# Twelve head pairs on one core: the copies of transposed keys move from SyncE's queue to GpSimd's

## The reference

```
h = rmsnorm(x, norm_g);  proj = h @ w_in          # q, k, v, gate of each group, forget logits
o_sb = stick_breaking_attention(q_sb, k_sb, v_sb)                       # causal
o_ch = chunked_relpos_attention(rmsnorm(q_ch), rmsnorm(k_ch), v_ch, rel_bias)   # own + 8 chunks of 64
o_fx = forgetting_attention(rmsnorm(q_fx), rmsnorm(k_fx), v_fx, log_sigmoid(f)) # causal
mixed = concat(o_sb * silu(g_sb), o_ch * silu(g_ch), o_fx * silu(g_fx))
out = x + mixed @ w_out
```

## Time and profile before

| | |
|---|---|
| device time, median of 3 runs | 1045.06 us |
| device time of the profiled execution | 1045.31 us |
| its span | 1043.5 us |
| PE busy | 1015.7 us, 97% |
| DVE, ACT busy | 682.6 us (65%), 632.2 us (61%) |
| POOL busy | 102.1 us, 10% |
| PE's share of the chain that ended last | 82% |
| copies stack<-stack, from issue to landing | 192 of 128 KB, median 2.3 us |

### The profile page before, as it was taken

One profiled execution on the slowest core, in us unless ns is written; L12 is line 12 of the kernel. 1 busy time (PEld: TensorE's weight loads), 2 busy tenths in 40 slices (PEclk: granted clock), 3 DMA queues, 4 the chain that ended last, 5 costly groups with the idle time before them and its releaser, 6 DMA issues.

```text
span 1043.5 us, 16263 instructions
## 1 busy us (share of the span) xinstructions
PE 1015.7 (97%) x5816; PEld 911.2 (87%) x5816; DVE 682.6 (65%) x1304; ACT 632.2 (61%) x1232; POOL 102.1 (10%) x90
## 2 busy tenths in 40 slices
PE   6999999999999999999999999999999998999998
PEld 6988989899899998998998998998998986787787
DVE  5656675765866667667557548879789787877100
ACT  6658775776767767758667667556567555553000
POOL 1210201101211011011012001011010010000000
PEclk9999999999999999999999999999999999999999
DMA  8254151431522513314314204204214228732941
GB/s 251 83 139 117 36 152 42 113 104 33 136 80 66 137 42 107 96 52 130 84 40 127 77 21 115 68 22 127 56 30 121 61 64 253 207 102 83 302 131 38
DMA packets 112944, 105.50 MB, mean 101 GB/s; under 512 B 10048, under 2 KB 83784, under 8 KB 112864
## 3 DMA queue, kind: packets, MB, share of 16 engines
q1 hardware_dynamic: 110784, 104.43, 36.3%
q10 hardware_dynamic: 2080, 0.04, 0.1%
HBM read 62.44 MB, written 19.98 MB: 79 GB/s over the span
## 4 chain that ended last, share of the span: by engine, by line
PE 82%; DVE 8%; DMA 4%; ACT 3%; issue 2%; SPq 0%; POOL 0%; ACTq 0%; DVEq 0%; POOLq 0%
PE psP L1216 37%; PE psO L1308 9%; PE psP L1220 8%; PE psT L1290 8%; PE psS L1268 4%; PE psS L1269 4%; PE psP L1356 2%; PE psS L1356 2%; PE psP L1326 2%; PE psT L1238 2%; PE psO L1356 2%; DVE big L1001 1%; DVE rb L1120 1%; PE psS L1273 1%; DMA stack<-mixed_scratch 1%
## 5 line engine op out<-in xcount | busy, mean ns | idle before, releaser
L1216 PE MATMUL psP<-big 128*128 128x384 f32 (+1 forms) x2304 | 478.5, 345 | 1.8 <-DVE big L1001 1.4
L1216 PEld LDWEIGHTS psP<-big 128*128 128x128 f32 x2304 | 394.9, 189 | 8.5 <-DVE big L1001 1.7
L1131 DVE TENSOR_TENSOR pt<-psT,pt 128x512 fp32r<-128x512 f32 (+1 forms) x224 | 143.4, 642 | 140.5 <-ACT pt L943 139.5
L943 ACT ACTIVATE pt<-psT 128x512 fp32r<-128x512 f32 (+1 forms) x224 | 125.1, 559 | 117.2 <-PE psT L1290 116.9
L1220 PE MATMUL psP<-big 128*128 128x512 f32 x576 | 157.1, 405 | 0.0
L1308 PE MATMUL psO<-pt,vst 128*128 128x512 f32 (+3 forms) x576 | 140.2, 343 | 6.3 <-DVE pt L1131 5.7
L1290 PE MATMUL psT<-identr,z 128*128 128x128 f32 x816 | 125.4, 272 | 0.0
L1220 PEld LDWEIGHTS psP<-big 128*128 128x128 f32 x576 | 102.4, 189 | 18.1
L1290 PEld LDWEIGHTS psT<-identr,z 128*128 128x128 f32 x816 | 101.6, 140 | 15.3
L1308 PEld LDWEIGHTS psO<-pt,vst 128*128 128x128 f32 x576 | 99.2, 189 | 17.8 <-issue 8.6
L1104 DVE CUSTOM_DVE_ANT_0 z<-psS,rb 128x640 f32<-128x640 f32 (+7 forms) x128 | 89.4, 699 | 35.7 <-PE psS L1269 17.3
(11 more groups left out here) (113 smaller groups left out, 1097.4 us busy)
## 6 DMA issues: line engine op xcount, KB each, us to landing
stack<-stack SPq DMA_DIRECT2D x192, 128.0 KB, 2.3
wraw<-in_w_in_dram SPq DMA_DIRECT2D x90, 192.0 KB, 2.6
wraw<-in_w_in_dram SPq DMA_DIRECT2D x24, 256.0 KB, 3.3
mixed_scratch<-mst SPq DMA_DIRECT2D x24, 256.0 KB, 2.4
mixed_scratch<-gate SPq DMA_DIRECT2D x24, 256.0 KB, 2.6
wraw<-in_w_out_dram SPq DMA_DIRECT2D x24, 256.0 KB, 3.2
rb<-decay_scratch SPq DMA_DIRECT2D x8, 512.0 KB, 4.1
big<-mixed_scratch SPq DMA_DIRECT2D x8, 512.0 KB, 6.1
```

Source lines behind the costliest of these rows:

```text
L943: nc.scalar.activation(pt[:, ci % PTR, 0, 0:w], psT[:, m % NT, 0:w], ACT.Copy).then_inc(s_hi, 1)
L1131: nc.vector.tensor_tensor(pt[:, ci % PTR, 1, 0:w], psT[:, m % NT, 0:w], pt[:, ci % PTR, 0, 0:w].bitcast(F32), ALU.subtract).then_inc(s_eva ...
L1216: ins = nc.tensor.matmul(dst[:, 0:TOKW - first], hT[a][:, k, i * P:(i + 1) * P], wpair[b][:, k, first:TOKW], start=(k == 0 and q == 0), st ...
```

## The change

The two copies of step `keys` are issued by GpSimd instead of SP. Their wait on `s_qh[s]`, their sizes, their semaphore and their place in the common list of steps are the same. All 48 blocks are concerned, 96 transfers.

```diff
@@ SP's program
-                if kind == "keys":
-
-                    _, j, s, u = step
-                    cols = slice(u * HALF, (u + 1) * HALF)
-                    sp.wait_ge(s_qh[s], 32 * (2 * j + u + 1))
-                    sp.dma_start(stack[0:HD, s, 1, cols].bitcast(F32), stack[HD:P, s, 1, cols].bitcast(F32)).then_inc(s_kh[s], 16)
-                    sp.dma_start(stack[0:HD, s, 2, cols].bitcast(F32), stack[HD:P, s, 2, cols].bitcast(F32)).then_inc(s_kh[s], 16)
@@ GpSimd's program
+                if kind == "keys":
+
+                    _, j, s, u = step
+                    cols = slice(u * HALF, (u + 1) * HALF)
+                    pool.wait_ge(s_qh[s], 32 * (2 * j + u + 1))
+                    pool.dma_start(stack[0:HD, s, 1, cols].bitcast(F32), stack[HD:P, s, 1, cols].bitcast(F32)).then_inc(s_kh[s], 16)
+                    pool.dma_start(stack[0:HD, s, 2, cols].bitcast(F32), stack[HD:P, s, 2, cols].bitcast(F32)).then_inc(s_kh[s], 16)
```

## The result

The changed kernel takes **1060.95 us** (median of 4 runs, 1060.4 to 1061.49), the kernel before took 1044.82 beside it (1043.54 to 1045.76): ratio 1.0145, 95% interval 1.0127 to 1.0163, so 16 us slower. The forecast was 1047.5 with a range of 1042.0 to 1056.0, so the measured time lies 5 us above the range. The interval says where the ratio of the two times lies with 95% confidence.

The account below looks back on a forecast made before the run. PE, busy 97% of the span, was taken as the bound. Stalls 4.5, traffic 1.5 and gate's weights 1.0 less the gain 4.6 gave +2.4 us, so 1047.5 us, range 1042.0 to 1056.0.

Parts of the forecast that it names:

- Removed from SP, the gain of 4.6 us: Last pair: chunk and `mixF` tile 1 go out earlier, 2.9 us of PE's wait and 1.7 us of low clock saved.
- rival 5: Last pair: the tile was not held by its place, so gain 0, sum +7.0, 1052 us; upper end of forecast's 0.47.
- GpSimd's issue at 1.04 us: Price of each key issue on GpSimd, taken from its product over 128 x 512; copies land 1.0 us later.
- The case to which I gave 0.15: Rival 1: issue on GpSimd near 0.61 us, decided by a price below about 0.8; 1042.2 us, chance 0.15.
- Stalls of 4.5 us from it: PE waits for keys landing 1.0 us later in blocks (0, 1) of pairs 0 to 4; pair 11's 0.1 rounded away.
- one of my signs of being wrong: The prediction is wrong if further blocks than the five near (0, 1) of pairs 0 to 4 come to wait.
- Traffic at 1.5 us: SP's next loads ahead of or beside the keys cost 0.3 us in each of five blocks; bounds 0 to 7.5.
- The gate's weights at 1.0: GpSimd's gate weights behind the copies of (1, 0) start ACT's line 813 0.65 us late, pairs 1 to 7; 1.0 us.
- Rival 3: GpSimd slow to issue, 1.64 us each: stalls 11.3 us, sum +16.4, 1061.5 us; chance 0.14.
- rival 4: DVE holds GpSimd up at every issue, 1.7 us each, time near 1062 us; chance 0.04.
- Rival 1: The freed SP wins: GpSimd's issue near 0.61 us, stalls 0.2, gain 4.6, sum -2.9, 1042.2 us; chance 0.15.
- another of my signs of being wrong: The prediction is wrong if `mixF` tile 1 in the last pair lands no earlier.

Follow-up runs that it names:

- e5: Against the kernel before: only block (0, 1) of the last pair, pair 11, has its key copies issued by GpSimd; 1048.94 us, ratio 1.0031.
- e10: The changed kernel, with SP held until a GpSimd memset placed ahead of its two key issues; 1062.07 us, ratio 1.0143 to the kernel before.
- e1: The changed kernel, with SP held at its old place until a GpSimd memset behind its two key issues; 1047.13 us, ratio 1.0006 to the kernel before.
- e8: Against the kernel before: only the blocks (0, 1) of pairs 0 to 4 have their key copies issued by GpSimd; 1057.25 us, ratio 1.0109.
- e4: Against the kernel before: the 36 blocks other than (0, 1) have their key copies issued by GpSimd; 1045.33 us, ratio 0.9996.

## Why the prediction was wrong

Each step as the prediction put it.

**Removed from SP, the gain of 4.6 us: failed, and with the wrong sign.** In e5 chunk and tile were issued 3.4 and 3.5 us earlier, as I had reckoned, and two things failed behind that. First, the tile did not land earlier: 875.86 in e5, 875.88 before. The 2.9 us that I took from its place in the list were nothing: it was not held by its place, as rival 5 has it and as my lower bound of 0 allowed. Second, the place that it took was that of the keys. In the sum I let 128 KB of keys delay the tile by 0.4 us and never asked what 1 MB of tile does to the keys: by the same division, 1 MB / 314 GB/s = 3.3 us, against the 0.9 us that pair 11 had to spare. Measured, the keys came 5.7 us later in e5 (8.5 after the queries, against 2.8), so the division is too small as well. e5 measured the whole step by itself: 3.2 us lost, not 4.6 gained, about half of it clock. This is 7.8 of the 13.5 us by which the forecast was short.

**GpSimd's issue at 1.04 us: mis-sized.** It is 0.52 to 0.56. A product on GpSimd is no measure of a transfer issued there. The case to which I gave 0.15, below 0.8, is the one that came. What remains of "later than SP" stands ahead of the issue: in pair 1 GpSimd's first issue starts 0.28 us behind the landing, SP's started 0.02 behind it, and in a quiet block the keys land about 3.1 us after the queries, against 2.82. It isn't GpSimd's waking: in e10 the memset starts 0.04 us behind the landing and the first issue 0.09 us, and the keys of quiet blocks land 2.8 to 2.9 us after the queries, as from SP. Why an issue that stands directly behind the wait starts later than that, no run shows.

The Trainium skill, "DMA: Bandwidth & Descriptors", section "Latency and other measured facts", which I had cited for 0.4 us more from GpSimd, came nearer in size: 0.28 us here. But it lies ahead of the issue, and from issue to landing the medians are the same from both engines.

**Stalls of 4.5 us from it: wrong reason and size, and one place too few.** Five of the six waits are in pairs 0 to 4, as foretold. The sixth and longest, 4.0 us, is in pair 11, which I had rounded away at 0.1: a further block that comes to wait was one of my signs of being wrong. e1 has the later issue with the order kept, and costs 0.06% with 1.3 us of wait. So the later issue is worth 0.5 us of wait and nothing that can be measured in the time (at most 0.24%, by the interval), not 4.5 us.

**Traffic at 1.5 us, bounds 0 to 7.5: mis-sized, the main miss.** e8 puts it and the path together, for the same five blocks, at 1.09% or 11.4 us, of which the longer waits are 8.4 and the rest mostly clock. The reasons for 0.3 a block were wrong in kind: a median near the minimum is that of 48 blocks, of which five count, and in those five the loads that SP was held back from stood directly behind the wait in its list. The upper bound left out the clock: I had reckoned with it where it was to be gained, in the last pair, and nowhere else.

**The gate's weights at 1.0: nothing.** ACT's line 813 waits for POOL 2.5 us in all, in three pieces, in the changed kernel; e4, with the copies of (1, 0) ahead of these weights, costs nothing.

**The rivals.** Rival 3 has the number (1061.5) and not the mechanism: its issue of 1.64 us is contradicted by every row (the longest of the 96 took 0.72), and so is rival 4's. Rival 1's condition, an issue below 0.8 us, was met, and its time of 1042 was off by 19: that a cheap issue decides was itself the mistake. Rival 5, the tile not held by its place, is right about the tile: 3.5 us earlier in the list brought it no earlier landing. Its time of 1052 was still 9 us short, since it says nothing of what the tile and the loads do to the keys. That the tile lands no earlier was another of my signs of being wrong.

The rule that I weighed and set aside, that a second issuing engine isn't a second set of DMA engines (the Trainium skill, "DMA: Bandwidth & Descriptors", section "Issuing engines are not separate DMA queues"), names the right resource. What I answered, that the wait is the queue's and not the engines', holds for the issue of the tile and not for its landing, and it shows only half: that wait also kept the loads off the engines while the keys passed.

What stays open: how large the head start must be. It lies between a load 0.04 us behind the second issue (lost, pair 3 of e10) and 0.66 us behind it (kept, e1), and no run was made between. In pair 3 the write of a finished output also stands 0.2 us nearer to the copies in e10 than in e1, which is not separated. That interleaving explains the whole delay of the keys in e10 is read from the packets of one pair, not tried by itself. In the stalls of pairs 2 to 4 I have read the same pattern but not taken each apart.

## What to carry to other kernels

A wait in front of a transfer on a shared queue does two things: it delays what stands behind it, and it keeps that traffic away from the transfer. Before you free such a queue, write down what will be issued in the gap, in bytes, and divide by the measured rate: the urgent copy loses that much or more (here 3.3 us by the division for the tile alone, 5.7 measured). A small copy that an engine waits for belongs ahead of the large loads; if it has to be issued from another engine, hold the loads until its last issue is over, not until what it waits for is there. And a wait that disappears from the list isn't a gain: compare the landings themselves.

And where waits come to about 2 us or more, count the clock that may fall with them: of the 16 us here, 6 were that.

## What the runs showed of the hardware

- A transfer of 64 rows by 512 columns issued by GpSimd costs it 0.52 to 0.56 us, and lands 2.3 to 2.4 us after issue (median), both as from SP. Its packets are in another queue and there are fewer of them: 4608 in q0, where q1 lost 110784 - 103104 = 7680.
- A transfer that stands directly behind a wait starts 0.28 us behind the landing on GpSimd and 0.02 us on SP. With a one-column memset between (e10) the memset starts 0.04 us and the transfer 0.09 us behind the landing.
- A load issued between 0.18 us ahead of the first copy and 0.04 us behind the second delays the landing of the keys although both copies are small: 4.9 to 6.5 us after the queries in pairs 1 to 3 of the changed kernel and of e10, against 4.2 to 4.5 in e1. In the window from 139.9 to 141.9, 96 packets of the copies pass in e1 and 35 in e10.
- Of two transfers of 512 KB from DRAM that were issued 3.5 us earlier in e5, the later one landed at the same time to 0.02 us (875.86 against 875.88).
- With waits of PE of 1.7 to 4.6 us the clock went to 0.50 for 3.4 or for 6.8 us, from inside the wait or up to 1.4 us behind it. Which of the two, the length of the wait does not tell: 2.15 us came with 6.8, 4.00 with 3.4, and 2.12 in pair 1 with none.
